# Pool mixers as products with scaled band matrices, turned tiles in two FFNs, and the last store on SyncE

## The chip, the cores and the metric

The kernel runs on one core of one Trainium2 chip. The metric is the device time of one execution in microseconds. Matrix products run on TensorE (PE in the profile), elementwise work on VectorE (DVE), ScalarE (ACT) and GpSimd (POOL); SyncE (SP) issues the loads. Each engine has its own queue of instructions, worked off in order, and they meet only at semaphores.

## The reference

One inference step of a trunk of 4 layers, for a prompt of 512 tokens and 8 sample tokens of one token each, 1024 channels, float32. Each layer is x = x + mixer(rmsnorm(x)) and x = x + swiglu(rmsnorm(x)). The mixers are pool, convolution, attention, pool. The pool mixer, which the change rewrites, is

```
u = rmsnorm(x, g)                       # rows; 15 rows of history come before a sample token
for group g, window w in (2, 4, 8, 16): # 4 groups of 256 channels
    mean = mean of the last w rows of u (of those there are)
    d[g] = mean - u
    y[g] = d[g] @ pool_w[g]             # 256 x 256
x = x + y * scale
state_p = last 15 rows of u (prompt);  state_s = history and u, last 15 rows (samples)
```

`swiglu(h)` is `(silu(h @ w_gate) * (h @ w_up)) @ w_down` with 2816 inner channels. The outputs are x at the end, for prompt and samples, the states of the pool and convolution layers, and rows of keys and values.

## The kernel before

**Layout.** x is kept with channels on partitions: 8 tiles of 128 channels by 520 tokens (512 of the prompt, then 8 samples). A float32 matrix product is made from three products of a faster type: both factors are split in a high and a low part, and low by low is left out (`half_products`, L487). A weight comes as `raw` (512 KB, loaded by SP), ScalarE makes `w_hi` (L925) and VectorE `w_lo` (L1264). A **unit** is the part of a weight that one slot holds, 48 products of 260 columns. The other factor is made likewise: after a tile of x is updated, ScalarE makes its square (L931) and the next input's `xin_hi` (L940), VectorE `xin_lo` (L1276), and POOL adds the squares up (L1738). `means` (L515) averages them over channels by products with a constant matrix, and ScalarE makes 1/rms by Ln and Exp (L945, L946), the same in all partitions, `rstd`.

**Order.** Every engine's program is written out by hand, in the same order of units and tiles; tables (`UNIT`, `TILE`, `TP`, `MIX`, `STORED`) give the counts that the waits use. `TP` numbers the **batches** of turned data: TensorE turns a tile by a product with the identity (`batch`, L534; `tails`, L566) into `bank6` or `bank7`, ScalarE copies it out (L950), and the next batch in that bank waits for that copy.

**Start.** SP loads the constants (561 KB), the samples, x in two halves of the channels, the weights of the first mixer and the history. POOL loads 15 rows of vectors (gains, biases), which are turned too, into `vec`. TensorE turns samples and 8 tiles of x, ScalarE copies and squares, VectorE adds up squares (L1700), `means(0)` and `rstd` follow, then `vec`.

**Pool mixer.** VectorE makes `hn` = x * gain * rstd, 8 tiles (L1287). The sample columns go with the turned history (L1293 to L1300). The window sums of `hn` are made by adding shifted copies, groups 0 and 1 on VectorE (L1313), 2 and 3 on POOL (`window_sums`); VectorE makes the difference to `hn` (L1321 to L1323). ScalarE rounds it to `mix_hi` (L970), VectorE makes `mix_lo` (L1329), and TensorE makes the group's 48 products, 24 for each tile of output. VectorE updates x (L1338), and the next input follows as above. TensorE also turns the last 23 columns of `hn` (L566) into `stage`, from which POOL stores the states.

**FFN.** 44 units for gate and up, two slots each step, and then 8 tiles of the down product with 3 units each. In the fourth FFN the output tile is turned by `y_tile`, tile c - 1 after tile c of four, and at the fourth tile of four both the third and the fourth:

```
                        if layer == 3:
                            if c:
                                y_tile(m0, i, c - 1)
                            if c == 3:
                                y_tile(m0, i, 3)
```

ScalarE copies it to `y_sb` (L950), and POOL stores it, 256 KB of the prompt (L1871) and 4 KB of the samples (L1874) a tile.

## Time and profile before

| | |
|---|---|
| median of 3 runs | 2254.21 us (2250.06 to 2254.46) |
| the profiled execution | 2252.45 us |
| its span | 2250.2 us |
| TensorE busy | 2102.0 us, 93% |
| VectorE, ScalarE, POOL busy | 1079.6, 952.1, 326.5 us |
| mean granted clock of TensorE | 0.975 of 2.4 GHz |
| MB, mean 90 GB/s |

Durations are read from the profiled execution; its time is 2.25 us more than its span. A row of a timeline has a start, a duration, the engine, the line of the kernel, the operation, what is written and read, and a count of instructions that follow one another; in brackets stands how long the engine was idle before, and what ended that. The records of products overlap, since they are pipelined: two that start 0.12 us apart are each 0.28 long. A float32 product that isn't split stands in the trace as two records.

### The profile page before, as it was taken

Reading aid. Unit: us, or ns where it says so; the run is one execution under the profiler, and the core shown is the slowest. Engines: PE = TensorE matmul, PEld = TensorE weight load, DVE = VectorE, ACT = ScalarE, POOL = GpSimd, SP = SyncE. Lnnn points to the kernel's source line nnn. Section 1 sums busy time; section 2 is a strip of 40 time slices with the busy share of each in tenths; the row PEclk is TensorE's granted clock in tenths of the full one; section 3 lists DMA queues with packets and bytes.
Section 4 is the critical chain, followed back from the end, with each engine's and each line's share of the span. In section 5 each row is a group of like instructions: output and inputs, shape, how many; then the busy total and the mean of one; then the engine's idle time right before and its main releaser. Section 6 shows DMA issues by size and latency. Waiting matters only on the chain. (4 is left out here: it accounts for less than half of the span.)

```text
span 2250.2 us, 41629 instructions
## 1 busy us (share of the span) xinstructions
PE 2102.0 (93%) x17072; PEld 2029.2 (90%) x17072; DVE 1079.6 (48%) x1446; ACT 952.1 (42%) x1280; POOL 326.5 (15%) x294
## 2 busy tenths in 40 slices
PE   2899999999889999999899979999999949999998
PEld 1899999999369999999899959999999939999998
DVE  5644443359955444433366655444432284444321
ACT  3543432255764434322477753443432234343221
POOL 4200000048921000000111114000000140000000
PEclk9999999999899999999999989999999969999999
DMA  4233332342003333322433252333332313333231
GB/s 135 68 92 93 93 90 86 96 103 75 29 22 89 90 93 93 91 86 77 150 113 102 69 205 76 88 93 93 90 89 87 88 30 91 87 92 93 87 106 52
DMA packets 345054, 201.53 MB, mean 90 GB/s; under 512 B 7465, under 2 KB 337481, under 8 KB 344932
## 3 DMA queue, kind: packets, MB, share of 16 engines
q1 hardware_dynamic: 341460, 193.21, 29.1%
q0 software_dynamic: 3504, 7.06, 1.1%
q8 instruction: 64, 1.05, 0.2%
q14 instruction: 26, 0.21, 0.0%
HBM read 193.51 MB, written 8.60 MB: 90 GB/s over the span
## 5 line engine op out<-in xcount | busy, mean ns | idle before, releaser
L487 PE MATMUL acc<-xin_hi,w_hi 128*128 128x260 f32 x3456 | 984.1, 285 | 11.0 <-issue 6.9
L487 PE MATMUL acc<-xin_hi,w_lo 128*128 128x260 f32 x3456 | 978.5, 283 | 0.0
L487 PE MATMUL acc<-xin_lo,w_hi 128*128 128x260 f32 x3456 | 975.5, 282 | 0.0
L925 ACT ACTIVATE w_hi<-raw 128x1024 fp32r<-128x1024 f32 (+1 forms) x332 | 344.9, 1039 | 992.1 <-PE acc L487 974.9
L487 PEld LDWEIGHTS acc<-xin_hi,w_hi 128*128 128x128 f32 x3456 | 652.4, 189 | 22.9 <-issue 17.9
L487 PEld LDWEIGHTS acc<-xin_lo,w_hi 128*128 128x128 f32 x3456 | 652.0, 189 | 0.3
L487 PEld LDWEIGHTS acc<-xin_hi,w_lo 128*128 128x128 f32 x3456 | 652.2, 189 | 0.0
L1264 DVE TENSOR_TENSOR w_lo<-raw,w_hi 128x1024 fp32r<-128x1024 f32 (+1 forms) x332 | 406.3, 1224 | 351.5 <-ACT w_hi L925 351.5
L487 PE MATMUL acc<-h_hi,w_hi 128*128 128x260 f32 x1408 | 397.9, 283 | 0.0
L487 PE MATMUL acc<-h_lo,w_hi 128*128 128x260 f32 x1408 | 397.9, 283 | 0.0
L487 PE MATMUL acc<-h_hi,w_lo 128*128 128x260 f32 x1408 | 397.5, 282 | 0.0
L487 PEld LDWEIGHTS acc<-h_hi,w_lo 128*128 128x128 f32 x1408 | 265.3, 188 | 0.0
L487 PEld LDWEIGHTS acc<-h_hi,w_hi 128*128 128x128 f32 x1408 | 264.9, 188 | 0.4 <-issue 0.3
L487 PEld LDWEIGHTS acc<-h_lo,w_hi 128*128 128x128 f32 x1408 | 264.9, 188 | 0.0
L1382 DVE TENSOR_TENSOR u_buf<-acc,rstd 128x520 f32<-128x520 f32 x88 | 61.6, 700 | 293.9 <-PE acc L487 293.9
L1379 DVE TENSOR_TENSOR g_buf<-acc,rstd 128x520 f32<-128x520 f32 x88 | 61.6, 700 | 227.9 <-PE acc L487 215.0
L487 PE MATMUL acc<-mix_hi,w_hi 128*128 128x260 f32 x320 | 98.2, 307 | 46.8 <-DVE x L1338 15.6
L1738 POOL TENSOR_TENSOR sqacc<-sqacc,sq 128x520 f32<-128x520 f32 x49 | 83.5, 1704 | 386.3 <-ACT sq L931 386.0
L1813 POOL TENSOR_TENSOR conv<-conv,prod_p 128x512 f32<-128x512 f32 x90 | 131.4, 1461 | 33.2 <-ACT prod_p L1031 21.3
L1735 POOL COPY sqacc<-sq 128x520 f32<-128x520 f32 x7 | 6.8, 966 | 870.8 <-ACT sq L931 870.8
L487 PEld LDWEIGHTS acc<-mix_hi,w_hi 128*128 128x128 f32 x320 | 66.3, 207 | 50.1 <-issue 47.2
L487 PE MATMUL acc<-mix_lo,w_hi 128*128 128x260 f32 x320 | 96.1, 300 | 0.0
(281 smaller groups left out, 1977.4 us busy)
## 6 DMA issues: line engine op xcount, KB each, us to landing
raw<-in_ffn_w_gate SPq DMA_DIRECT2D x88, 512.0 KB, 3.9
raw<-in_ffn_w_up SPq DMA_DIRECT2D x88, 512.0 KB, 3.9
raw<-in_ffn_w_down SPq DMA_DIRECT2D x64, 512.0 KB, 4.1
raw<-in_ffn_w_down SPq DMA_DIRECT2D x32, 384.0 KB, 3.5
raw<-in_attn_w_qkv SPq DMA_DIRECT2D x24, 512.0 KB, 3.9
raw<-in_conv_w_in SPq DMA_DIRECT2D x16, 512.0 KB, 4.0
raw<-in_conv_w_out SPq DMA_DIRECT2D x8, 512.0 KB, 4.1
in_mix<-in_cache_k SPq DMA_DIRECT2D x8, 512.0 KB, 5.1
```

Source lines behind the costliest of these rows:

```text
L487: last = pe.matmul(acc[:, b, 0:HALF], w[:, w_tile * P:(w_tile + 1) * P], v[:, h * HALF:(h + 1) * HALF], start=start and t == 0, stop=stop ...
L925: act.activation(w_hi[n.slot(2)][:, 0:cols], raw[:, n.slot(4), 0:cols], ACT.Copy).then_inc(split_hi, 1)
L1264: dve.tensor_tensor(w_lo[n.slot(2)][:, 0:cols], raw[:, n.slot(4), 0:cols], w_hi[n.slot(2)][:, 0:cols].bitcast(F32), ALU.subtract).then_inc ...
L1379: dve.tensor_tensor(halves(g_buf[:, c, :]), accumulator(m), halves(rstd[:]), ALU.mult).then_inc(evacuated, 1)
L1382: dve.tensor_tensor(halves(u_buf[:]), accumulator(m + 1), halves(rstd[:]), ALU.mult).then_inc(evacuated, 1)
L1735: pool_e.tensor_copy(sqacc[:], sq[:, 0, :]).then_inc(sq_added, 1)
L1738: pool_e.tensor_tensor(sqacc[:], sqacc[:], sq[:, m % 2, :], ALU.add).then_inc(sq_added, 1)
L1813: pool_e.tensor_tensor(out, out, prod_p[:, p % 3, :], ALU.add).then_inc(prod_added, 1)
```

## The change

A pool mixer no longer normalizes x in its layout by channels. It takes x with **tokens on partitions**, in 4 blocks of 128 tokens (the rows as they come from memory for the first mixer; for the second, tiles that TensorE turns in the third FFN). A window mean minus the token is a product over tokens with a **band matrix**: for a window it holds 1/w on w diagonals, less 1 on the main one, 128 rows by 128 + 16 columns, the last for what reaches into the next block. The 1/rms of a token is a factor of a row of that matrix, so the band matrices are scaled by it, four blocks by four windows. The gain of a channel is applied when the product is copied out as `mix_hi` and `mix_lo`. Edge, history and samples have small matrices of their own.

- **SP**: 64 KB of the constants first, x in four blocks of tokens, the band matrices (360 KB); the other constants last. Bands and history of the second mixer are loaded in the third FFN, ahead of that mixer's weights. SP issues the stores of the last output tile.
- **1/rms of tokens**: the first mixer squares and sums rows of x (two blocks and the samples on ScalarE, two on VectorE); in the second `token_means` makes 5 small products. Then Sqrt on ScalarE and a reciprocal on VectorE. The root of blocks 0 and 1 scales bands on ScalarE, 2 and 3 on VectorE.
- **TensorE**: `bands(m)` for a tile of 128 channels, 4 products of 128 columns and 3 of w columns, unsplit float32, into one of two banks; `samples()`, 16 products of 8 columns; the groups' products as before. The order is bands 0, 1, samples, bands 2, 3, group 0, bands 4, 5, group 1, bands 6, 7, groups 2, 3. In the first mixer the turns of the tiles 5 to 7 of x (`start_tile`) stand between.
- **VectorE**: `hn`, sample sums, window sums and differences go. It scales bands, makes `mix_lo` by tile, and two rows of state of 1024 elements, which POOL stores. POOL's window sums go, too. The first sum of squares and `means(0)` go; scalars for attention are made in the first FFN.
- **Third and fourth FFN**: tile c - 1 is turned after the first of the three units of tile c (`turn_tile`), tile 7 at the end; ScalarE copies it at the end of tile c.

The core of the diff:

```diff
+        t, p = np.arange(BAND)[None, :], np.arange(P)[:, None]
+        seen = (t >= p) & (t < p + win)
+        own = (t == p).astype(np.float32)
+        bands[:, B_MAIN + BAND * g:B_MAIN + BAND * (g + 1)] = np.where(seen, 1.0 / win, 0.0) - own
+        bands[:, B_EDGE + 16 * g:B_EDGE + 16 * g + 16] = (np.where(seen, 1.0 / np.minimum(t + 1, win), 0.0) - own)[:, 0:16]
+        for b in range(DEC):
+            bands[HIST_P * b + HIST_P - (win - 1):HIST_P * (b + 1), B_HIST + DEC * g + b] = 1.0 / win
+            bands[b, B_SMP + DEC * g + b] = 1.0 / win - 1.0
...
+            sp.dma_start(const[:, 0:P], shape_constants[:, 0:P]).then_inc(ident_in, 16)
+            sp.dma_start(xs_rows[:], x_sample[:, 0, :]).then_inc(rows_in[4], 16)
+            for b in range(4):
+                sp.dma_start(x_rows[:, b, :], x_prompt[0, b * P:(b + 1) * P, :]).then_inc(rows_in[b], 16)
+            sp.dma_start(band_c[:], shape_constants[:, N_CONST:N_CONST + N_BAND]).then_inc(bands_in, 16)
             load_pool(0)
             sp.dma_start(hist_rows[:], state_pool[0].rearrange("b j d -> (b j) d")).then_inc(hist_in, 16)
+            for rows in (slice(0, DEC), slice(96, P)):
+                sp.dma_start(gain_rows[rows, :], norm_mix[0].partition_broadcast(rows.stop - rows.start)).then_inc(gains_in[0], 16)
+            sp.dma_start(const[:, P:N_CONST], shape_constants[:, P:N_CONST]).then_inc(consts_in, 16)
...
+            sp.wait_ge(units_done, UNIT["ffn2"] + 2 * FT)
+            sp.dma_start(band_l[:], shape_constants[:, N_CONST:N_CONST + N_BAND]).then_inc(bands_in, 16)
+            sp.dma_start(hist_l[:], state_pool[1].rearrange("b j d -> (b j) d")).then_inc(hist_in, 16)
             load_pool(1)
...
             load_ffn(3)
+            tb = TP["end"] + 2 * (KT - 1)
+            sp.wait_ge(tp_taken, tb + 1)
+            sp.dma_start(y_prompt[0].rearrange("(b p) c -> p b c", p=P)[:, :, D - P:D],
+                         y_sb[:, KT - 1, 0:SEQ].rearrange("p (b c) -> p b c", b=4)).then_inc(last_stored, 16)
+            sp.wait_ge(tp_taken, tb + 2)
+            sp.dma_start(y_sample[:, 0, D - P:D], y_sb[0:DEC, KT - 1, SEQ:SEQ + P]).then_inc(last_stored, 16)
...
+            def token_means():
+
+                pe.wait_ge(sq_added, 8 * 6)
+                pe.wait_ge(rstd_ready, 6)
+                for b in range(4):
+                    pe.matmul(pair[:, 1, 2 * b:2 * b + 2], sqacc[:, b * P:(b + 1) * P], avg[:, 0:2], start=True, stop=True)
+                pe.matmul(pair[0:DEC, 1, 8:10], sqacc[:, SEQ:T], avg[:, 0:2], start=True, stop=True).then_inc(mean_ready, 1)
...
+                def bands(m):
+                    g, win = m // 2, WINDOWS[m // 2]
+                    if m < 2:
+                        pe.wait_ge(band_act, 2 * q + 2)
+                        pe.wait_ge(band_dve, 3 * q + 3)
+                    else:
+                        pe.wait_ge(mix_lo_ok, mix + m - 1 + (m > 3))
+                    cols = slice(m * P, (m + 1) * P)
+                    for b in range(4):
+                        last = pe.matmul(pair[:, m % 2, b * P:(b + 1) * P], x_tok[:, b, cols], band_s[:, b, g, 0:P],
+                                         start=True, stop=b == 0)
+                        if b:
+                            last = pe.matmul(pair[:, m % 2, b * P:b * P + win], x_tok[:, b - 1, cols], band_s[:, b - 1, g, P:P + win],
+                                             start=False, stop=True)
+                    last.then_inc(band_full, 1)
+
+                def samples():
+                    pe.wait_ge(hist_in, 16 if q == 0 else 64)
+                    pe.wait_ge(bands_in, 16 * q + 16)
+                    pe.wait_ge(tp_taken, TP["end"] if q else 3)
+                    for m in range(KT):
+                        cols, here = slice(m * P, (m + 1) * P), DEC * (m // 2)
+                        pe.matmul(bank7[:, DEC * m:DEC * (m + 1)], xs_tok[0:DEC, cols], smp_diag[:, here:here + DEC],
+                                  start=True, stop=True)
+                        last = pe.matmul(bank7[:, 64 + DEC * m:64 + DEC * (m + 1)], hist[:, cols],
+                                         band[0:DEC * HIST_P, B_HIST + here:B_HIST + here + DEC], start=True, stop=True)
+                    last.then_inc(smp_full, 1)
...
+                if q:
+                    token_means()
+                bands(0)
+                bands(1)
+                samples()
+                bands(2)
+                bands(3)
+                if q == 0:
+                    pe.wait_ge(smp_ready, 1)
+                    start_tile(7, 5, bank7, 3)
+                group(0)
+                if q == 0:
+                    start_tile(8, 6, bank6, 7)
+                bands(4)
+                bands(5)
+                group(1)
+                if q == 0:
+                    start_tile(9, 7, bank7, 8)
+                bands(6)
+                bands(7)
+                group(2)
+                group(3)
...
+                            if layer >= 2 and j == 0 and i + c:
+                                turn_tile(layer, m0, 4 * i + c - 1)
...
+                def high(m):
+                    act.wait_ge(band_full, 8 * q + m + 1)
+                    act.activation(mix_hi[:, m, 0:SEQ], pair[:, m % 2, :], ACT.Copy, scale=vec[:, gain + m:gain + m + 1])\
+                       .then_inc(mix_hi_ok, 1)
...
+                    act.activation(tok[0:DEC, ROOT + 4:ROOT + 5], pair[0:DEC, 1, 8:9], ACT.Sqrt, bias=eps[0:DEC]).then_inc(root_ready, 1)
+                act.wait_ge(rstd_ready, 6 * q + 1)
+                act.wait_ge(bands_in, 16 * q + 16)
+                main = band[:, B_MAIN:B_MAIN + 4 * BAND].rearrange("p (g t) -> p g t", g=4)
+                act.activation(band_s[:, 0, :, 16:BAND], main[:, :, 16:BAND], ACT.Copy, scale=tok[:, RSTD:RSTD + 1])
+                act.activation(band_s[:, 0, :, 0:16], band[:, B_EDGE:B_EDGE + 64].rearrange("p (g t) -> p g t", g=4), ACT.Copy,
+                               scale=tok[:, RSTD:RSTD + 1]).then_inc(band_act, 1)
+                act.activation(band_s[:, 1], main, ACT.Copy, scale=tok[:, RSTD + 1:RSTD + 2]).then_inc(band_act, 1)
...
+                def low(m):
+                    dve.wait_ge(mix_hi_ok, mix + m + 1 + (m > 1))
+                    dve.scalar_tensor_tensor(mix_lo[:, m, 0:SEQ], pair[:, m % 2, :], vec[:, gain + m:gain + m + 1],
+                                             mix_hi[:, m, 0:SEQ].bitcast(F32), ALU.mult, ALU.subtract).then_inc(mix_lo_ok, 1)
...
+                dve.wait_ge(root_ready, q + 1)
+                dve.reciprocal(tok[:, RSTD:RSTD + 4], tok[:, ROOT:ROOT + 4])
+                dve.reciprocal(tok[0:DEC, RSTD + 4:RSTD + 5], tok[0:DEC, ROOT + 4:ROOT + 5]).then_inc(rstd_ready, 1)
+                dve.wait_ge(rstd_ready, 6 * q + 1)
+                dve.wait_ge(bands_in, 16 * q + 16)
+                main = band[:, B_MAIN:B_MAIN + 4 * BAND].rearrange("p (g t) -> p g t", g=4)
...
+                for b in range(2, 4):
+                    dve.tensor_scalar(band_s[:, b], main, tok[:, RSTD + b:RSTD + b + 1], None, ALU.mult).then_inc(band_dve, 1)
+                low(0)
+                low(1)
...
+                                       vec[:, gain:gain + KT].unsqueeze(2).to_broadcast([P, KT, DEC]), ALU.mult))
+                dve.tensor_tensor(smp_diff[:], smp_own[:], bank7[:, 64:128].rearrange("p (k b) -> p k b", k=KT), ALU.add)\
...
+                                                 accum_out=lam_tmp[:, QK + j:QK + j + 1]).then_inc(lam_sums, 1)
+                        dve.wait_ge(lam_sums, j + 1)
+                dve.wait_ge(gains_in[q], 32)
+                if q == 0:
+                    dve.wait_ge(rows_in[4], 16)
+                else:
+                    dve.wait_ge(tp_taken, TP["end"])
+                x_tok, xs_tok, _, _, out = POOL_IN[q]
+                for here, rows, col in ((slice(96, P), x_tok[96:P, 3, :], 3), (slice(0, DEC), xs_tok[:], 4)):
+                    dve.scalar_tensor_tensor(out[here, :], rows, tok[here, RSTD + col:RSTD + col + 1], gain_rows[here, :],
+                                             ALU.mult, ALU.mult).then_inc(state_ready, 1)
+                update(0)
+                update(1)
+                low(4)
+                low(5)
+                low_next(0)
+                low_next(1)
+                update(2)
+                update(3)
+                low(6)
+                low(7)
+                low_next(2)
+                low_next(3)
+                for m in (4, 6):
+                    update(m)
+                    update(m + 1)
+                    low_next(m)
+                    low_next(m + 1)
...
+                pool_e.dma_start(pool_state_p[q, 0], out[P - HIST_P:P, :]).then_inc(stored, 16)
+                pool_e.dma_start(pool_state_s[q, :, HIST_P - 1, :], out[0:DEC, :]).then_inc(stored, 16)
 
```

What the order of VectorE's instructions is at the start of the second mixer, before (`hn`, then the sample columns, window sum and difference of the first group):

```order
L1284 MEMSET hn 128x8x16 [waits rstd_ready]
L1285 MEMSET wsum 128x4x16
L1287 SCALAR_TENSOR_TENSOR hn<-x,vec,rstd 128x520 x8
L1293 COPY hist_s<-hn 128x64 [waits tp_taken,hn_ready,pads_ready]
L1296 TENSOR_REDUCE last_s<-hist_s 128x16 [waits dve_seq]
L1296 TENSOR_REDUCE last_s<-hist_s 128x16 x3
L1300 SCALAR_TENSOR_TENSOR diff<-last_s,hn 128x2x8 [waits dve_seq]
L1300 SCALAR_TENSOR_TENSOR diff<-last_s,hn 128x2x8 x3
L1313 TENSOR_TENSOR wsum<-hn 128x2x512
L1321 TENSOR_TENSOR edge<-wsum,const 128x32 [waits dve_seq]
L1322 TENSOR_TENSOR diff<-edge,hn 128x2x16 [waits dve_seq]
L1323 SCALAR_TENSOR_TENSOR diff<-wsum,hn 128x2x496
```

and in the changed kernel, up to the first update of x:

```order
L1477 RECIPROCAL tok<-tok 128x4 [waits root_ready]
L1478 RECIPROCAL tok<-tok 8x1
L1482 TENSOR_SCALAR smp_diag<-band_l,tok 8x32 [waits bands_in,rstd_ready]
L1485 TENSOR_SCALAR band_s<-band_l,tok 128x576 x2
L1450 SCALAR_TENSOR_TENSOR mix_lo<-pair,vec,mix_hi 128x512 [waits mix_hi_ok] x2
L1491 TENSOR_TENSOR smp_own<-bank,vec 128x64 [waits smp_full]
L1493 TENSOR_TENSOR smp_diff<-smp_own,bank 128x64 [waits dve_seq]
L1497 TENSOR_TENSOR mix_lo<-smp_diff,mix_hi 128x8x8 [waits mix_hi_ok,smp_ready]
L1450 SCALAR_TENSOR_TENSOR mix_lo<-pair,vec,mix_hi 128x512 [waits mix_hi_ok] x2
L1516 SCALAR_TENSOR_TENSOR rows_l<-x_turned,tok,gain_rows 32x1024 [waits tp_taken,gains_in1]
L1516 SCALAR_TENSOR_TENSOR rows_l<-xs_l,tok,gain_rows 8x1024
L1461 SCALAR_TENSOR_TENSOR x<-acc,vec,x 128x520 [waits tile_done] x2
```

The work on whole tiles of x is gone, and low parts and state rows stand in its place ahead of the first update. TensorE at the same place, before (the means, turned history, the turned last columns of `hn`, the first group):

```order
L515 MATMUL pair<-sqacc,avg 128x260 [waits rstd_ready,sq_added]
L515 MATMUL pair<-sqacc,avg 128x260
L534 MATMUL bank<-const,hist_rows 128x120 [waits tp_taken,hist_in]
L534 MATMUL bank<-const,hist_rows 128x120 x3
L534 MATMUL bank<-const,hist_rows 128x120 [waits tp_taken]
L534 MATMUL bank<-const,hist_rows 128x120 x3
L566 MATMUL bank<-const,hn 23x128 [waits tp_taken,hn_ready]
```

and now (the turned last tile of x, the means per token, the first band tile):

```order
L700 MATMUL bank<-const,x 128x128 [waits tp_taken,evacuated]
L700 MATMUL bank<-const,x 128x128 x3
L703 MATMUL bank<-const,x 8x128 [waits tp_taken]
L574 MATMUL pair<-avg,sqacc 128x2 [waits rstd_ready,sq_added]
L574 MATMUL pair<-avg,sqacc 128x2 x3
L575 MATMUL pair<-avg,sqacc 8x2
L590 MATMUL pair<-band_s,x_turned 128x128 [waits band_dve,band_act]
L590 MATMUL pair<-band_s,x_turned 128x128
L593 MATMUL pair<-band_s,x_turned 128x2
L590 MATMUL pair<-band_s,x_turned 128x128
```

TensorE's wait on `hn` is gone; it waits on the scaled bands of ScalarE and VectorE. At the end of the last FFN TensorE had, before, two output tiles behind the last product:

```order
L598 MATMUL bank<-const,x_out 128x128 [waits tp_taken]
L598 MATMUL bank<-const,x_out 128x128 x3
L600 REGISTER_ALU
L601 MATMUL bank<-const,x_out 8x128 [waits tp_taken]
L594 REGISTER_ALU
L596 REGISTER_ALU [waits evacuated]
```

and now has one:

```order
L520 MATMUL acc<-h_lo,w_hi_58 128x260
L520 MATMUL acc<-h_hi,w_lo_60 128x260
L700 MATMUL bank<-const,x_out 128x128 [waits tp_taken,evacuated]
L700 MATMUL bank<-const,x_out 128x128 x3
L703 MATMUL bank<-const,x_out 8x128 [waits tp_taken]
```

The other one stands behind the first unit of the last tile.

## Rows read from the trace of the kernel before

**Rows 1.** The page, part 1: busy time of each engine, its share, its instructions.
```profile
PE 2102.0 (93%) x17072; PEld 2029.2 (90%) x17072; DVE 1079.6 (48%) x1446; ACT 952.1 (42%) x1280; POOL 326.5 (15%) x294
```
**Rows 2.** TensorE's waits, 0 to 100 us: line, what for, total, times, longest.
```profile
PE bank L566 <- DVE hn L1287: 13.5, 1, 13.5
...
PE bank L534 <- DMA x_rows<-in_x_prompt: 9.8, 1, 9.8
```
**Rows 3.** TensorE's waits, 1786 to 1900 us, with the second mixer.
```profile
PE bank L566 <- DVE hn L1287: 15.0, 1, 15.0
PE acc L487 <- issue: 10.4, 1, 10.4
```
**Rows 4.** Timeline of the second mixer: start, duration, instruction; ScalarE, POOL, VectorE.
```profile
1793.15 1.06 ACT L925 ACTIVATE w_hi<-raw 128x1024 fp32r<-128x1024 f32 x1 [3.25 <-PE acc L487]
...
1794.84 1.28 ACT L945 ACT_TABLE_LOAD   x1
...
1794.89 1.70 POOL L1738 TENSOR_TENSOR sqacc<-sqacc,sq 128x520 f32<-128x520 f32 x1 [14.07 <-ACT sq L931]
...
1801.68 13.57 DVE L1287 SCALAR_TENSOR_TENSOR hn<-x,vec,rstd 128x520 f32<-128x520 f32 x8
...
1819.63 1.21 DVE L1313 TENSOR_TENSOR wsum<-hn 128x1024 f32<-128x1024 f32 x1
...
1830.57 0.76 DVE L1338 SCALAR_TENSOR_TENSOR x<-acc,vec,x 128x520 f32<-128x520 f32 x1 [1.85 <-PE acc L487]
...
1857.01 2.46 DVE L1276 SCALAR_TENSOR_TENSOR xin_lo<-x,vec,xin_hi 128x520 fp32r<-128x520 f32 x2
```
**Rows 5.** Timeline of VectorE, first mixer: the first update of x.
```profile
60.34 0.76 DVE L1338 SCALAR_TENSOR_TENSOR x<-acc,vec,x 128x520 f32<-128x520 f32 x1 [1.98 <-PE acc L487]
```
**Rows 6.** Stretches of the second mixer: engines' busy time, granted clock, DMA share, GB/s.
```profile
core 0: us, PE busy (x) PEld busy (x) DVE busy (x) ACT busy (x) POOL busy (x), PEclk, DMA share, GB/s
...
1796.00:1827.60 31.60, 5.61 (x21) 4.00 (x21) 25.75 (x30) 6.96 (x10) 17.39 (x11) 0.50 0.30 71
1832.00:1834.00 2.00, 2.00 (x16) 2.00 (x15) 0.96 (x3) 0.83 (x3) 0.62 (x1) 0.84 0.00 0
1827.60:1857.50 29.90, 21.63 (x126) 21.05 (x126) 22.53 (x26) 14.27 (x21) 10.81 (x8) 0.74 0.06 19
```
**Rows 7.** f32 products: timeline at 1353 us; by line at 1794:1800 and 1857.5:1861 (busy us, mean ns).
```profile
1352.97 0.61 PE L842 MATMUL bank<-s_dec,select 128*128 128x1 f32 x4 [1.31 <-DVE select L1657]
1353.44 0.80 PE L846 MATMUL bank<-select,s_dec 128*128 128x128 f32 x5
...
L515 PE MATMUL pair<-sqacc,avg 128*128 128x260 f32 x4 | 2.1, 680 | 3.5 <-POOL sqacc L1738 3.5
...
L515 PE MATMUL pair<-sqacc,avg 128*128 128x260 f32 x4 | 1.1, 401 | 0.8 <-issue 0.8
```
**Rows 8.** Turned tiles by line over the span: the input's, the output's.
```profile
L534 PE MATMUL bank<-const,x_rows 128*128 128x128 f32 x32 | 8.5, 431 | 0.2
...
L598 PE MATMUL bank<-const,x_out 128*128 128x128 f32 x32 | 4.9, 276 | 1.7 <-ACT y_sb L950 1.7
```
**Rows 9.** ScalarE by line: a scaled copy of 512 elements out of PSUM.
```profile
L1131 ACT ACTIVATE mix_hi<-acc,sub_gain 128x512 fp32r<-128x512 f32 x8 | 5.2, 683 | 7.0 <-PE acc L720 7.0
```
**Rows 10.** The last vector row: POOL's issue, and the issues' KB and median us to landing.
```profile
8.90 0.48 POOL L1795 DMA_DIRECT2D vec_rows<-in_attn_subln  x1
...
vec_rows<-in_attn_subln POOLq DMA_DIRECT2D x1, 0.5 KB, 5.6
```
**Rows 11.** Timelines around turned output tiles, POOL's last issue, and landing of such stores.
```profile
2139.81 0.28 PE L487 MATMUL acc<-h_hi,w_lo 128*128 128x260 f32 x1
...
2140.59 0.28 PE L487 MATMUL acc<-h_lo,w_hi 128*128 128x260 f32 x1
...
2172.55 0.28 PE L487 MATMUL acc<-h_hi,w_lo 128*128 128x260 f32 x1
...
2174.52 0.66 PE L598 MATMUL bank<-const,x_out 128*128 128x128 f32 x4 [1.15 <-ACT y_sb L950]
...
2175.52 0.28 PE L487 MATMUL acc<-h_lo,w_hi 128*128 128x260 f32 x1
...
2243.45 0.51 POOL L1874 DMA_DIRECT2D out_y_sample<-y_sb  x1
...
out_y_sample<-y_sb POOLq DMA_DIRECT2D x8, 4.0 KB, 3.5
```

More of the change, by code:

```diff
@@ L369, in halves @@
             return t.rearrange("p (h c) -> p h c", h=2)
[L372 removed]
+        TP = {"start": 0, "conv": 10, "pool1": 16, "end": 32}
         @block.sync
@@ L1867, in _ @@
                 add_squares(6)
-            for m in range(KT):
+            for m in range(KT - 1):
                 tb = TP["end"] + 2 * m
```

442 lines of the change are left out of this document (221 added, 221 removed).

## The prediction

> **What bounds the kernel now.** I read the page first: TensorE is busy 93% of the span [rows 1]. In the FFN phases its 260-column products stand 0.12 us apart without a gap, so a change pays only where TensorE stands still, and costs where it puts work into those streams. The waits of the engine, by line, say where it stands still. In the first 100 us it waits 9.8 us for the rows of x and 13.5 for `hn` [rows 2]; in the second pool mixer 15.0 for `hn`, and 10.4 in the row called "issue", which stands ahead of the first group's products, while VectorE makes differences and low parts [rows 3]. The timeline says what fills these waits: VectorE makes `hn` for 13.57 us, then sample and window parts, and the first update of x, which needs the first group's products, starts at 1830.57 in the second mixer [rows 4] and at 60.34 in the first [rows 5]. Both mixers are a chain over VectorE.
>
> **Second mixer, to the first update.** Zero is 1793.15, where TensorE ends the third FFN and ScalarE starts its last split. In the change ScalarE does that split (1.06), a turned pair of copies and a square (0.7 each, by its 0.68 for 512 elements), and POOL its last add (1.70) [rows 4, 9]: 4.1 us. Then the means per token, 5 small f32 products. An f32 product is two records. Four records of one column take 0.61 us with the tail of the last, and five of 128 columns 0.80; the first of the five starts 0.47 after the first of the four. So records stand 0.12 us apart whatever the width, 0.235 a product [rows 7], at full clock. In the idle stretch ahead of the first group the granted clock is 0.50 [rows 6], the lower of the two levels (1.2 GHz), and the two L515 products take 2.1 us there against 1.1 later [rows 7]: twice the price. So 5 x 0.47 = 2.2, now 6.4. Two roots on ScalarE (estimate 0.2 each) and two reciprocals (about as much): 7.2. ScalarE scales two band matrices by 1/rms, 576 elements each, one in two pieces: by its 0.68 [rows 9] 1.5, now 8.7. VectorE scales the other two beside it.
>
> Now TensorE starts on the bands. A tile is 4 products of 128 columns and 3 of 2 to 16, 7 x 0.235 = 1.65 us, at the low clock 3.3. Bands 0 and 1 come after a long pause, so 6.6: 15.3. After that I take full clock, since before the change it had a mean of 0.84 between 4 and 6 us from the first group's start [rows 6]. Samples, 16 x 0.235 = 3.8: 19.1. Bands 2 and 3, 3.3: 22.4. High and low part of band 3, 0.68 on ScalarE and 0.75 on VectorE: 23.8. Group 0 needs only bands 0 and 1, and its first tile (12 products, 1.4 us) is done by then, but VectorE has two state rows of 1024 elements ahead of the first update, 1.21 each by the nearest row [rows 4]: 26.2. Before it was 37.4. **Gain 11.2.** `hn`, window sums and differences are gone from VectorE and POOL. A table load (1.28 before [rows 4]) fits under POOL's add and the means. The loads of bands and history, 840 KB, are issued in the third FFN, ahead of the mixer's weights on SP's queue, and TensorE waits for no weight in [rows 3]. POOL loads the gains for the state rows behind its last add (1.70 [rows 4]), two issues, and by the 5.6 of such loads [rows 10] they are there at about 11, needed at 23.8. POOL's two stores stand ahead of its first add and end about 1.2 after the state rows, when the first square is due.
>
> **Second mixer, from there on.** From the first update to the end of the last low part of the next input it was 1859.47 - 1830.57 = 28.9 us [rows 4]. VectorE now has 8 updates (5.6), 4 low parts (3.0), 8 low parts of the next input (9.4) and 2 splits (2.4) = 20.4, and waits, since group 3 cannot start until bands 6 and 7 went through ScalarE and VectorE. I count 7 us of waits: 27.4. **Gain 1.5.** Bounds: none, and 4.
>
> **First mixer.** It starts when `vec` is there, which high and low parts need. The last of its rows is issued by POOL at 8.90 and lands 5.6 later: 14.5 [rows 10]. The rows of x should be earlier: the constants ahead of them are now 64 KB, not 561. TensorE turns `vec` (0.7) and four tiles of x, 16 turns of 0.22 (twice the 0.11 of the output's turns, see below): 18.7. Bands 0 and 1 at low clock 6.6: 25.3. Samples 3.8, bands 2 and 3 3.3, high and low 1.4: 33.8. Then on VectorE a split with its wait 1.4, lambda sums 0.7, state rows 2.4: 38.4. Before: 60.34. **Gain 21.9**, and 1.0 behind it, as above. The sum of squares on VectorE, `means(0)` and the Ln and Exp are within this gain. The lambda scalars are now made in the first FFN, where VectorE waits for TensorE.
>
> The 32 turns of x took 431 ns each, those of the output 276 [rows 8], though TensorE was busy nearly without pause around the former; they ran at the low clock. The Trainium skill, "TensorE: Matmul & The Clock Gate", Part 4: PE-mode transpose, says that turns don't count as work for the clock; the trace agrees with it. If they did count, bands 0 and 1 of the first mixer would run at full clock and the time would be 3.3 us less, 2217.
>
> **Third FFN.** TensorE is full there, so turned tiles are added time. One pair (five turns) moves the next products by 0.54: 2140.59 less 2139.81 less two steps of 0.12 [rows 11]. Seven stand in the stream, the eighth in the gap before the mixer. **Loss 3.8.** ScalarE's 16 copies lie in its idle time. Each turn comes after a unit of 5.74 us, and its update takes 0.7, so none is late.
>
> **Fourth FFN.** At the fourth tile two tiles were turned in a row, and the second waited for ScalarE: 2175.52 less 2172.55 less two steps is 2.73, for 1.08 of work [rows 11]. The stall of 1.65 goes; at the end one tile moves from behind the last product into the stream, 0.54. **Gain 1.1.**
>
> **Tail.** POOL's last issue ends at 2243.96, behind three others of 0.8 and 0.5 in a row [rows 11]. Two issues are left at the end, by SyncE: gain 1.1 (1.3 less what the second turn hid). What follows, 6.2 us to the end of the span, holds a landing; the median of these stores is 3.5 [rows 11], and SyncE's may be as long or half of that, 0 to 1.8; I take 0.4, near none, as nothing shows a faster one. **Gain 1.5.** The Trainium skill, "DMA: Bandwidth & Descriptors", has hardware queues start sooner than POOL's; no run here shows it for a store.
>
> **Sum.** -11.2 - 1.5 - 21.9 - 1.0 + 3.8 - 1.1 - 1.5 = -34.4. The profiled run took 2252.45, so 2218.05; the median of the runs shown, 2254.21, is 1.76 more: **2220 us**. A difference of 0.2% (4.5 us) is about the least that a measurement of this kernel tells from none.
>
> **Rivals.**
> *The clock stays low through both mixers (slower).* Between bands, samples and groups TensorE waits for ScalarE and VectorE. If that holds the clock at 1.2 GHz, samples (3.8), bands 2 and 3 (3.3) and some 10 of the 18 us behind them (four bands, 96 group products) are added again on the path, 17 a mixer: the whole gain. If the first unit of the FFN runs so too, 5.7 more each: 2220 + 34 + 11 = **2265**. It decides from 17 us of added low-clock work a mixer. Against it: the clock had a mean of 0.74 from the first group on, with idle time between groups [rows 6]. Chance 0.05.
> *Low for part of them.* Samples and bands 2, 3 doubled, 7 us a mixer: **2234**. For it: that same 0.74 says that it takes long to rise, or falls between. Chance 0.13.
> *Late start.* The loads share the queues with 360 KB of bands and the pool weights, and `vec` or the last block comes at 20 to 22, not 14.5: **2226**. Chance 0.08.
> *Narrow products nearly free.* If products of 2 to 16 columns cost by their columns, 6.3 us a mixer on the path would go: **2207**. Records of one column at the same step as those of 128 speak against it [rows 7]. Chance 0.03. The Trainium skill, the same TensorE page, Back-to-back issue gap, gives such narrow products less than half the gap of 128 columns, while its LDWEIGHTS section lets the weight load set a floor; the rows side with the latter.
> *No change*, **2254**: the change moves the chain from `hn` to bands, high parts and state rows, and these give all of it back. Against it: `hn` alone is 13.57 us of the path and the whole new chain to the first update 26.2. Chance 0.03.
>
> **The numbers.** Forecast 0.68. The range takes in the bounds of the landing (1.4 below), 2.5 more behind each first update, full clock in bands 0 and 1 (-6.6) with the partly low clock above: 2212 to 2236. Faster 0.92, same 0.03, slower 0.05.
>
> **What would show it.** In the profile after: no `hn` row; first updates near 38 and 1800 (the second mixer's zero near 1774); clock low over bands 0 and 1 and full by the samples; turns in the third FFN of 276 ns with no wait; no wait at the fourth tile of the last FFN; SyncE's stores right behind the last copy. I would be wrong if the bands' records stood further apart than 0.12 at full clock, if the clock stayed at 0.50 past the samples, or if `vec` came after 16 us.

## Result: 2218.8 us, and the profile after

| | before | changed |
|---|---|---|
| median | 2252.89 us (4 runs, 2250.06 to 2254.46) | 2218.84 us (4 runs, 2215.9 to 2222.4) |
| ratio to before | | 0.9854, 95% interval 0.9841 to 0.9866 |
| profiled execution, span | 2250.2 us | 2215.9 us |

The forecast was 2220. By sections, each from one row of either trace to the next, it came out like this (ends of a section: first `u_buf` of the first FFN, `rstd` of the third, last update of x in the third, first `u_buf` of the fourth, last update of `x_out`, end of the span):

| section | before | changed | difference | forecast |
|---|---|---|---|---|
| start, first mixer | 96.59 | 74.11 | -22.5 | -22.9 |
| two FFNs, convolution, attention | 1419.57 | 1396.09 | -1.0 | 0 |
| third FFN | 1793.27 | 1773.52 | +3.7 | +3.8 |
| second mixer | 1867.38 | 1839.53 | -8.1 | -12.7 |
| fourth FFN | 2240.00 | 2210.97 | -1.2 | -1.1 |
| tail | 2250.2 | 2215.9 | -5.3 | -1.5 |

(Columns 2 and 3 are times in the trace, the difference is that of the section's length.) The total is right because errors cancelled: the second mixer gave 4.6 us less than forecast, the tail 3.8 more.

Not all of the first mixer's gain is the chain on VectorE. Before, `hn` started at 29.12:

```profile
29.12 13.57 DVE L1287 SCALAR_TENSOR_TENSOR hn<-x,vec,rstd 128x520 f32<-128x520 f32 x8
```

In the changed kernel the first product of the bands starts at 19.57, and the first update comes at 40.69 and not at 60.34. So 9.5 of these 19.6 us were won ahead of the chain, by the earlier rows of x, the sum of squares and `means(0)` that went, and the earlier `vec`; no run takes these apart. In the second mixer 1.3 us were won ahead of the chain (8.4 to 7.1 from the last update of the third FFN), and 4.4 in it (28.9 to 24.5).

The page of the changed kernel, part 1, which answers to [rows 1]:

```profile
PE 2135.3 (96%) x17370; PEld 2067.8 (93%) x17370; DVE 1029.6 (46%) x1402; ACT 949.2 (43%) x1298; POOL 290.8 (13%) x278
```

TensorE's waits in its first 100 us, which answer to [rows 2]:

```profile
PE bank L998 <- DMA vec_rows<-in_attn_subln: 5.2, 1, 5.2
PE acc L654 <- DMA x_rows<-in_x_prompt: 4.1, 4, 1.2
...
PE acc L520 <- DVE x L1461: 2.9, 1, 2.9
```

and from 1760 to 1880, which answer to [rows 3]:

```profile
PE pair L590 <- ACT band_s L1095: 2.4, 1, 2.4
PE acc L520 <- DVE x L1461: 2.1, 1, 2.1
PE acc L520 <- issue: 1.8, 1, 1.8
PE bank L700 <- ACT xs_l L1053: 1.8, 1, 1.8
```

The waits of 13 to 15 us for `hn` are gone, and no wait of these two stretches is longer than 5.2. TensorE is seldom idle in a mixer any more, and still the second one takes 66 us (1773.52 to 1839.53). The timeline of TensorE in the changed kernel's second mixer stands where [rows 4] did:

```profile
1777.08 1.05 PE L574 MATMUL pair<-avg,sqacc 128*128 128x2 f32 x8 [1.20 <-POOL sqacc L1896]
...
1780.66 1.22 PE L590 MATMUL pair<-band_s,x_turned 128*128 128x128 f32 x4 [2.39 <-ACT band_s L1095]
...
1786.72 0.59 PE L603 MATMUL bank<-smp_diag,xs_l 8*128 8x8 f32 x2
1787.24 0.60 PE L605 MATMUL bank<-band_l,hist_l 120*128 120x8 f32 x2
...
1795.02 1.20 PE L590 MATMUL pair<-band_s,x_turned 128*128 128x128 f32 x4
...
1800.99 0.57 PE L520 MATMUL acc<-mix_hi,w_hi 128*128 128x260 f32 x1
```

and that of VectorE has the first update:

```profile
1805.19 0.74 DVE L1461 SCALAR_TENSOR_TENSOR x<-acc,vec,x 128x520 f32<-128x520 f32 x1
```

The stretches of the second mixer (columns as in [rows 6]; the third number from the end is the granted clock) say where the time is:

```profile
1776.00:1778.00 2.00, 0.92 (x8) 0.92 (x8) 0.00 (x0) 1.83 (x3) 2.00 (x3) 1.00 0.47 131
1782.00:1784.00 2.00, 2.00 (x10) 2.00 (x11) 0.00 (x0) 0.16 (x1) 0.00 (x0) 0.50 0.00 0
1790.00:1792.00 2.00, 2.00 (x9) 1.90 (x9) 0.00 (x0) 0.00 (x0) 0.00 (x0) 0.50 0.00 0
1802.00:1804.00 2.00, 2.00 (x11) 2.00 (x11) 1.94 (x3) 0.00 (x0) 0.00 (x0) 0.50 0.00 0
1806.00:1808.00 2.00, 2.00 (x20) 2.00 (x19) 0.76 (x1) 2.00 (x4) 1.32 (x4) 1.00 0.30 47
```

and those of the first mixer:

```profile
24.00:26.00 2.00, 2.00 (x14) 1.87 (x14) 1.74 (x2) 1.47 (x3) 0.00 (x0) 1.00 0.57 241
...
28.00:30.00 2.00, 2.00 (x11) 1.98 (x10) 0.67 (x3) 0.63 (x2) 0.00 (x0) 0.50 0.85 221
...
38.00:40.00 2.00, 2.00 (x20) 2.00 (x19) 1.93 (x4) 0.00 (x0) 0.00 (x0) 1.00 0.50 138
```

TensorE is shown busy in all of each stretch from 1782 on, and the clock stays at 0.50 through 20 us of bands and samples. It is up by 1806, behind 260-column products that began at 1800.99. In the first mixer it was up over most of bands 0 and 1 and fell during the samples, at about 27.6. (Up to 20 us the column gives 1.00 too, but there the records stand as far apart as at the low level, 12 turned blocks in 2.56 us from 16.16 on; from 20.4 on they stand as at the full level. So for the start the spacing is the better witness.) The tail answers to [rows 11]: SyncE's two issues end at 2213.89, and 2.0 us later the span ends, where after POOL's it took 6.2. VectorE's last update:

```profile
2210.97 0.70 DVE L1579 TENSOR_TENSOR x_out<-acc,x 128x520 f32<-128x520 f32 x1 [8.73 <-PE acc L520]
```

The last issues on SyncE's queue:

```profile
2213.05 0.40 SPq L505 DMA_DIRECT2D out_y_prompt<-y_sb  x1
2213.49 0.40 SPq L508 DMA_DIRECT2D out_y_sample<-y_sb  x1
```

### The profile page after: what moved, and what is told of

It reads as the page before. It is cut to its first block, busy times and chain, and to the rows that moved or that the text cites. A ratio compares the mean times of both kernels' runs of the same rounds, so it can differ in the third digit from the quotient of the medians.

```text
span 2215.9 us, 42085 instructions
## 1 busy us (share of the span) xinstructions
PE 2135.3 (96%) x17370; PEld 2067.8 (93%) x17370; DVE 1029.6 (46%) x1402; ACT 949.2 (43%) x1298; POOL 290.8 (13%) x278
## 4 chain that ended last, share of the span: by engine, by line
PE 88%; POOL 4%; ACT 3%; DVE 3%; issue 2%; DMA 0%; POOLq 0%; ACTq 0%; DVEq 0%
PE acc L520 80%; POOL conv L1963 3%; PE pair L794 1%; PE pair L590 1%; PE bank L814 1%; PE pair L769 1%; DVE pair L1614 1%; ACT w_hi L1028 0%; PE acc L727 0%; PE pair L963 0%; PE acc L849 0%; PE bank L804 0%; ACT s_buf L1285 0%; PE acc L838 0%; PE pair L746 0%
## 5 line engine op out<-in xcount | busy, mean ns | idle before, releaser
L520 PE MATMUL acc<-mix_hi,w_lo 128*128 128x260 f32 x320 | 93.4, 292 | 0.0
```

Source lines behind the costliest of these rows:

```text
L520: last = pe.matmul(acc[:, b, 0:HALF], w[:, w_tile * P:(w_tile + 1) * P], v[:, h * HALF:(h + 1) * HALF], start=start and t == 0, stop=stop ...
```

## The experiments

Each starts from the changed kernel. Where one profile is compared, the sections matter more than the total: the middle of the program (first `g_buf` of the first FFN to the last update of x in the third), which no edit touches, was between 1699.7 and 1704.4 us long in these traces, so that totals can differ by 4.7 us for nothing that was edited. The table gives, from each trace: first update of x in the first mixer (A); first `g_buf` of the first FFN (B); last update of x in the third FFN to the first update in the second mixer (C), and to the first `g_buf` of the fourth FFN (D); last update of `x_out` to the end (E). The time is the median, with the number of runs.

| kernel | A | B | C | D | E | time |
|---|---|---|---|---|---|---|
| before | 60.3 | 91.6 | 37.3 | 69.1 | 10.2 | 2252.9 (4) |
| changed | 40.7 | 70.3 | 31.7 | 61.0 | 4.9 | 2218.8 (4) |
| e1, last store by POOL | 40.4 | 70.0 | 31.7 | 60.8 | 10.0 | 2223.1 (4) |
| e2, no narrow products | 35.6 | 65.4 | 26.6 | 55.0 | 5.0 | 2203.3 (1) |
| e3, turns ahead | 40.5 | 70.6 | 31.7 | 60.6 | 4.9 | 2217.5 (1) |
| e4, fillers in the pauses | 40.8 | 70.5 | 27.8 | 56.2 | 5.0 | 2212.1 (4) |
| e5, history apart | 38.3 | 67.9 | 28.3 | 57.1 | 5.0 | 2209.4 (1) |
| e6, state rows later | 41.0 | 72.8 | 30.5 | 61.5 | 4.9 | 2219.3 (1) |
| e7, vec by ScalarE | 37.1 | 66.8 | 31.7 | 61.0 | 4.9 | 2215.4 (1) |
| e8, e4 to e7 together | 39.5 | 70.4 | 25.1 | 54.8 | 4.9 | 2211.9 (4) |
| e9, fillers in the samples | 43.2 | 72.9 | 28.8 | 58.0 | 5.0 | 2217.6 (4) |
| e10, e9 and vec | 42.5 | 72.2 | 29.7 | 58.1 | 4.9 | 2214.6 (5) |
| e11, last store by ScalarE | 40.8 | 70.4 | 32.0 | 60.9 | 5.0 | 2217.4 (1) |
| e12, grouped | 39.4 | 69.1 | 26.2 | 54.6 | 4.9 | 2206.8 (5) |

### The tail: e1 and e11

```diff
-            for m in range(KT - 1):
+            for m in range(KT):
                 tb = TP["end"] + 2 * m
                 pool_e.wait_ge(tp_taken, tb + 1)
                 pool_e.dma_start(y_prompt[0].rearrange("(b p) c -> p b c", p=P)[:, :, m * P:(m + 1) * P],
```

(and SyncE's two stores left out.)

> The changed kernel with the stores of the last output tile issued by POOL again, all else as changed. The changed kernel ended 5.2 us after its last product started, the kernel before 10.5 us. Theory A (the end of the program waits longer for stores that POOL issued, whatever their length): the span grows by 3 to 5 us, to about 2220, with nothing moved by DMA in its last 4 us. Theory B (as predicted: only the longer issues and a slightly later landing): it grows by 0.5 to 1.5 us, to about 2217.

E is 10.0 again, all of the 5 us. That also answers what the two fewer issues were worth, since e1 has them too: 0.2 us (10.2 to 10.0), for POOL waits for ScalarE's copy anyway. POOL's issues in e1:

```profile
2211.50 0.79 POOL L2015 DMA_DIRECT2D out_y_prompt<-y_sb  x1 [9.98 <-ACT y_sb L1046]
2212.28 0.52 POOL L2018 DMA_DIRECT2D out_y_sample<-y_sb  x1
```

and how long such stores took there, from issue to landing (median us, last column):

```profile
out_y_prompt<-y_sb POOLq DMA_DIRECT2D x1, 256.0 KB, 2.7
out_y_sample<-y_sb POOLq DMA_DIRECT2D x1, 4.0 KB, 2.2
```

The second lands 2.2 us after its issue, at 2214.5, and the span ends at 2219.2: 4.7 us in which no DMA moves anything. That is what theory A had forecast. e11 has the two stores issued by ScalarE behind its last copy, and not by SyncE:

> The changed kernel with the last output tile's two stores issued by ScalarE, which makes the copy, and not by SyncE. From the last update of x_out to the end of the span it was 10.2 us in the kernel before, 10.0 in e1 (POOL), 4.9 in the changed kernel (SyncE). Theory A (late stores that POOL issued cost 5 us at the end; the other queues don't): 4.8 to 5.1. Theory B (it is SyncE's queue that is fast, for instance since SyncE itself waits for the end): 6 us or more.

5.0. So it is not SyncE that is fast; it is late stores by POOL that are followed by a long end. In the changed kernel POOL's last issue ends at 2203.3, 12.6 us before the end, and nothing of the kind follows. What the program waits for in these 4.7 us isn't shown by any row and stays open.

### The clock: e2, e3, e4

e2 leaves out the three narrow products of a band tile (`if b:` becomes `if False:`), so that its outputs lack what reaches in from the block of tokens before:

> The changed kernel without the 3 narrow products of each band tile (the first rows of a block of tokens then lack what reaches in from the block before). In the second mixer the clock stayed at 0.50 for 20 us of bands and samples. Theory N (the narrow products thin out the stream so that the clock is not raised): with 128-column products alone the granted clock rises within bands 0 and 1 or soon after them, and the first update comes some 5 us earlier than by the removed work alone. Theory S (unsplit float32 products do not raise it at all, or the samples hold it down): the clock stays at 0.50 until the first group, and only the narrow products' own time goes, 24 x 0.28 = 6.7 us over both mixers at the low clock, less at the full one: about 2212.

By A and C both mixers reach the first update 5.1 us earlier, where theory S gives 3.4. TensorE's timeline in the second mixer of e2:

```profile
1772.24 3.79 PE L590 MATMUL pair<-band_s,x_turned 128*128 128x128 f32 x16 [2.40 <-ACT band_s L1095]
1775.95 0.59 PE L603 MATMUL bank<-smp_diag,xs_l 8*128 8x8 f32 x2
...
1784.25 3.35 PE L590 MATMUL pair<-band_s,x_turned 128*128 128x128 f32 x16
1787.36 0.36 PE L520 MATMUL acc<-mix_hi,w_hi 128*128 128x260 f32 x1
```

and the stretches of the same:

```profile
1784.00:1786.00 2.00, 2.00 (x10) 2.00 (x11) 0.67 (x3) 0.26 (x1) 0.00 (x0) 0.50 0.00 0
1786.00:1788.00 2.00, 2.00 (x15) 2.00 (x15) 0.75 (x1) 1.05 (x2) 0.00 (x0) 0.74 0.00 0
1788.00:1790.00 2.00, 2.00 (x19) 2.00 (x18) 1.60 (x2) 0.33 (x1) 0.00 (x0) 1.00 0.00 0
```

It did not rise over bands 0 and 1, 3.7 us long here, nor over the samples; it rose at about 1787.0, 2.8 us into bands 2 and 3, so that group 0 starts at full clock. In the first mixer it rose within bands 2 and 3 too (at about 29.2). With nothing narrow between them, unsplit float32 products of 128 columns were followed by a rise in both mixers: theory N, but later than it said, and why bands 0 and 1 were not enough isn't shown. The gain itself doesn't decide for N. Most of it is the narrow products' own time: at the low clock a pair of tiles takes 3.7 us and not 6.06, 2.35 less, so 4.7 of the 5.1 for two pairs; theory S had them too cheap, at 3.4.

e3 sets 24 turned blocks ahead of the bands of the second mixer, where no pause interrupts them:

```diff
                     token_means()
+                    pe.wait_ge(band_act, 2 * q + 2)
+                    pe.wait_ge(band_dve, 3 * q + 3)
+                    for k in range(24):
+                        pe.transpose(pair[:, 0, (k % 4) * P:(k % 4 + 1) * P], x[:, k % 8, 0:P], ident)
```

> The changed kernel with 24 more turned blocks of 128 columns ahead of the bands of the second mixer, in one uninterrupted stream (their result is overwritten). At the low clock they take 24 x 0.21 = 5.1 us. Theory T (turned blocks count as work for the clock; in the first mixer it rose about 5 us after TensorE began on vec and x without a pause): the clock rises by the end of them, bands 0 and 1 run at 1.5 us a tile, not 3.0, and the 5.1 us are mostly given back: 2216 to 2219. Theory P (they do not count, as I wrote in the prediction): the clock stays at 0.50 until the first group and the time grows by 5.1: about 2222.

The stretches of e3's second mixer:

```profile
1782.00:1784.00 2.00, 2.00 (x11) 2.00 (x10) 0.00 (x0) 0.00 (x0) 0.00 (x0) 0.50 0.00 0
1784.00:1786.00 2.00, 2.00 (x20) 2.00 (x18) 0.00 (x0) 0.00 (x0) 0.00 (x0) 0.93 0.00 0
...
1794.00:1796.00 2.00, 2.00 (x9) 1.95 (x10) 0.45 (x2) 0.07 (x1) 0.00 (x0) 0.50 0.00 0
```

The clock rises during the turns, at about 1784.3, 2.8 us after they began, and with 4 us of added work C and the time are what they were. Theory T holds: **24 turned blocks in a row did raise the clock**, against what I wrote in the prediction and against the Trainium skill, "TensorE: Matmul & The Clock Gate", Part 4: PE-mode transpose; here the measurement decides. Then it falls again, during the samples.

e4 fills the pauses ahead of the second mixer's bands:

```diff
+            def fill(n):
+                w = w_hi[UNIT["pool1"] % 2]
+                for _ in range(n):
+                    pe.matmul(pair[:, 0, 0:HALF], w[:, 0:P], w[:, 0:HALF], start=True, stop=True)
...
+                    fill(10)
                     token_means()
+                    fill(18)
```

(and 14 ahead of the last turned tile.)

> The changed kernel with 42 products of 260 columns (fast type, result overwritten) put into the three stretches in which TensorE stands still between the end of the third FFN and the bands of the second mixer (14 ahead of the last turned tile, 10 behind it, 18 behind the means per token). Theory F (the low clock there is the price of the pause): the granted clock is 1.00 when the bands begin, bands 0 and 1 take 1.5 us a tile and samples 5, and the first update comes 5 to 9 us earlier: 2208 to 2212. Theory S (bands and samples cannot hold the clock, as in the first mixer, where it fell during the samples): bands 0 and 1 and most of the samples run at full clock, then it falls, and the gain is 4 to 6 us: 2211 to 2213. If fillers do not matter: 2217.

The stretches of e4's, over bands and in the samples:

```profile
1782.00:1784.00 2.00, 2.00 (x20) 2.00 (x19) 0.68 (x1) 0.69 (x1) 0.00 (x0) 1.00 0.03 8
1784.00:1786.00 2.00, 2.00 (x15) 1.88 (x13) 0.82 (x2) 0.69 (x1) 0.00 (x0) 0.91 0.00 0
...
1788.00:1790.00 2.00, 2.00 (x9) 1.90 (x10) 0.00 (x0) 0.00 (x0) 0.00 (x0) 0.50 0.00 0
```

C is 3.8 shorter, D 4.8, the time 2212.1 (2211.0 to 2214.7, all four below the changed kernel's fastest run of 2215.9; the intervals of the ratio touch at 0.984). So 42 products whose result nobody reads make the kernel faster, since they stand where TensorE waited anyway; of the 6.7 us between the medians, 1.9 are outside the section that was edited. The expectation for theory S is the one that came true: full clock over bands 0 and 1, then it fell, though sooner than expected, 1.6 us after the samples began.

### The samples: e5, e9

e5 takes the loop over 16 alternating products apart, 8 for the history and 8 for the tokens:

> The changed kernel with the 16 sample products split in two runs of 8: in the second mixer the history half stands behind the means per token, where TensorE waits 2.4 us for the scaled bands; in the first it stands between bands 0 and bands 1. Theory N (a long run of narrow products makes the clock fall: 3.7 us after the samples began in the first mixer, with 5 us of samples in a row): in the first mixer the clock does not fall, bands 2 and 3 take 1.5 us a tile, not 3.0, the first product of group 0 is at full clock, and the first update comes 3 to 5 us earlier. Theory S (8-column products of any grouping make it fall): no change in the first mixer. In the second mixer, where all is at the low clock anyway, 2.4 us of the waiting are used in both: together 2211 to 2213 by N, 2216 by S.

The gain is there (A 2.4, C 3.4, 2209.4), and the reason was another. The clock fell in the first mixer too, at about 25.5, and bands 2 and 3 ran at 3.0 us a tile, against what theory N had forecast. But a run of products of one kind is cheaper. TensorE's timeline in e5's first mixer has the two runs:

```profile
20.60 1.93 PE L603 MATMUL bank<-band_c,hist_rows 120*128 120x8 f32 x16
22.39 0.69 PE L590 MATMUL pair<-band_s,x_rows 128*128 128x128 f32 x4
...
24.02 2.29 PE L609 MATMUL bank<-smp_diag,xs_rows 8*128 8x8 f32 x16
```

and that of the changed kernel the alternating ones, at full clock too:

```profile
24.18 0.39 PE L605 MATMUL bank<-band_c,hist_rows 120*128 120x8 f32 x2
24.50 0.38 PE L603 MATMUL bank<-smp_diag,xs_rows 8*128 8x8 f32 x2
24.82 0.39 PE L605 MATMUL bank<-band_c,hist_rows 120*128 120x8 f32 x2
```

16 records of history take 1.79 us, 0.224 a product; alternating, a product takes 0.315. At the low clock it is 0.43 against 0.52. In the first mixer that is 1.4 us of A's 2.4 (samples and history take 4.0 and not 5.4); the rest is that the clock was up a little sooner. In the second, what stands between the bands is 3.5 us long and not 8.3, and the bands begin 1.4 later, behind the history: 3.4. Which difference between the two kinds of product makes alternating dearer (8 against 120 rows, or another) was not taken apart.

e9 is e4 with dense work among the samples (behind each pair two products of 260 columns in the second mixer, two turned blocks in the first):

> The fillers of e4 in the pauses ahead of the second mixer's bands, and now also fillers among the sample products of both mixers: behind each pair 2 products of 260 columns in the second mixer, 2 turned blocks of 128 columns in the first (8 x 0.24 and 8 x 0.22 us at full clock, 1.9 and 1.8 a mixer). Theory N (the samples' thin stream makes the clock fall; dense work among them holds it): clock at 1.00 from the first bands to group 0 in both mixers; bands 2 and 3 take 1.5 us a tile, group 0's first products stand 0.12 apart. Against e4 the second mixer's first update comes about 4 us earlier (23.5 after the end of the third FFN), the first mixer's about 4 earlier (36.5): 2204 to 2207. Theory S (samples and bands make it fall whatever stands among them): it falls within the samples, and the fillers' own time is added: 2213 to 2216.

2217.6, above both ranges. In the second mixer the clock holds longer than in e4, for 5.1 us of the samples (they begin at 1786.5 here) and not 1.6, and falls all the same before bands 2 and 3. The stretches of e9:

```profile
1788.00:1790.00 2.00, 2.00 (x17) 1.90 (x15) 0.08 (x1) 0.00 (x0) 0.00 (x0) 1.00 0.00 0
1790.00:1792.00 2.00, 2.00 (x14) 1.91 (x13) 0.00 (x0) 0.00 (x0) 0.00 (x0) 0.89 0.00 0
...
1794.00:1796.00 2.00, 2.00 (x10) 2.00 (x11) 0.65 (x3) 0.26 (x1) 0.00 (x0) 0.50 0.00 0
```

That the fillers held it is not shown. In the first mixers of the changed kernel, e1, e3, e4, e6 and e11, which have no filler and the same work up to there, the clock fell 1.3 to 4.3 us after the samples began, and in e9's, with turned blocks among them, after 3.9. What is shown is that this much did not keep it up, and cost its own time. More wasn't tried.

### The order on VectorE, and the start: e6, e7

> The changed kernel with VectorE's two state rows moved: in the first mixer behind its last low part, in the second behind the second update. In the first mixer they stand between low part and first update, which comes at 40.69 though the products are there at 38.1. Theory D (VectorE is the chain there, as I priced it): the first update comes 2.4 us earlier in the first mixer, up to 1.5 in the second, and some 3 us of it reach the end: 2215 to 2216. Theory G (bands, groups and the waits behind them set the pace, and VectorE's order does not matter): the first updates move, the first input of the FFN does not: 2218.

The end is as theory G says, 2219.3, but not since VectorE's order is of no matter. In the first mixer A did not move, because in this run the clock fell about 2.5 us earlier (25.0 for 27.6) and the last low part ahead of group 0 came at 38.07, not 35.55. That moment differs from run to run. Counted from that low part the first update did come 2.2 us sooner (2.9 for 5.1), and the first `g_buf` at the same 34.8: behind the mixer's last low part the state rows end at 70.8, and VectorE's lambda scalars and first `g_buf` come behind them. In the second mixer C is 1.2 shorter and D is not. So at these two new places the 2.4 us are paid again; whether another place would be free wasn't tried.

> The changed kernel with five of the 15 vector rows issued by ScalarE, which stands still then, and not as the last five by POOL. TensorE waits 5.2 us for the last of them, to 15.47. If the chain of the first mixer begins there, as I priced it: vec is there at about 12.5 (POOL's last issue ends at 6.9), and all that follows moves 2.5 to 3 us ahead: about 2216. If another load is late next (bands at about 11.5, the history at 17.7 for the samples, pool weights for group 0): less than 1 us, 2218.

A and B are 3.6 shorter: `vec` is turned at 11.9, not 15.5, and all follows. It is the one edit at the start that paid what it was priced at, and a little more (3.6 for 2.5 to 3).

### Putting them together: e8, e10, e12

> The three edits together, and the fillers of the second mixer (14 and 10, none behind the means per token, since the history half stands there). If the gains add up: fillers 6.5, samples in halves 4 or more, state rows 3, vector rows 2.5, less what overlaps: 2203 to 2206. Theory N says that in the second mixer the clock stays at 1.00 through bands 0 to 3 and group 0. Theory S says that it falls in the second half of the samples: 2208 to 2210.

2211.9, slower than either range, with four runs from 2207.3 to 2217.3. The second mixer is the best but one (D 54.8), though the clock fell at about 1780.4, within the first tile of bands, sooner than either theory had it. But the first lost what e5 and e7 had won: with `vec` 3.6 us earlier, the history run that e5 had put between bands 0 and bands 1 waited 2.2 us for its load, and the clock was at 0.50 from 20 on.

> e9 and the five vector rows by ScalarE of e7. If the gains add up, 3 us under e9: 2201 to 2204. If an earlier start meets a late load (the history lands at 17.7, the samples would begin at about 19.5), 1 us under e9 at most.

2214.6, 3 us under e9 as in the first clause, whose 2201 to 2204 had counted on e9's expected time; the section that changed, A, moved by 0.7 only, so the difference is not shown to be from there.

> What paid, without what did not: history products and sample products as two runs of 8 (in e5 such a run took 0.112 us a record at full clock where alternating operands of 8 and of 120 rows took 0.157), in the first mixer one behind the other after bands 1 (so that an earlier start does not wait for the history), in the second the history half behind the means; the fillers ahead of the second mixer; the five vector rows by ScalarE. State rows as in the changed kernel, no fillers among the samples. By sections: first input of the first FFN at about 65 to 67 (changed kernel 70.3), 54.8 to 56 from the end of the third FFN to the first input of the fourth (61.0), the rest as it was: 2204 to 2209, below e4's 2212. If the parts compete instead (clock falling sooner as in e8): 2210 to 2213.

e12 takes 2206.8 us (5 runs, 2205.8 to 2211.6; ratio to before 0.9804, interval 0.979 to 0.9817, apart from the changed kernel's 0.9841 to 0.9866): faster than both kernels. D is 54.6 as expected, B is 69.1 and not 65 to 67: the samples waited 0.7 us for the history, and their 16 products ran mostly at the low clock.

## Why the prediction was right, and where it was not

- **What bounds it**: right. `hn` and what followed on VectorE were the chain, and went. In the first mixer about half of the gain came ahead of that chain, which the forecast had in its sum as well.
- **Second mixer, up to the bands**: 7.2 us and not 8.7. "5 x 0.47 = 2.2" for the means failed (the product is 2.35, and the sum goes on with that): they took 1.2, since the clock was still up (1776:1778 at 1.00).
- **"After that I take full clock"**: the step that failed. Samples took 8.3, not 3.8, bands 2 and 3 6.0, not 3.3; the first update came at 31.7, not 26.2. I had read from [rows 6] that the clock rises within a few us once TensorE is busy; the rows were of 260-column products, and I took them for any work. In e2 and e3 it rose over 128-column work; in the changed kernel it did not rise in 20 us with narrow products between. My rival "low for part of them", with samples and bands 2 and 3 doubled, is what happened in this mixer. It added 7.2 us here and 4.3 in the first mixer. That the forecast of the total was met all the same is luck: the tail, the bands 0 and 1 of the first mixer, the means and what came behind the first updates were each cheaper than priced, and together gave these 11.5 us back.
- **"Records stand 0.12 us apart whatever the width"** [rows 7]: right for 128-column tiles with their narrow products (1.5 us at full clock, 3.0 at low, for my 1.65 and 3.3), wrong for the samples, 0.157 at full clock while the two kinds alternate and 0.112 when they don't (e5).
- **First mixer**: 40.7, not 38.4. `vec` was turned at 15.5 for my 14.5; bands 0 and 1 ran mostly at full clock (3.7 for 6.6); samples took 5.4, bands 2 and 3 6.0. Behind the first update, to the first `u_buf`, the first mixer was 1.8 us shorter than I had priced and the second 1.0.
- **Turned blocks and the clock**: wrong, by e3. The 32 turns of x before stood 0.27 us apart (8.75 us for all), with ScalarE's copies and squares between them, those of the changed kernel and of e3 0.21 at the low level, without a pause; I took the first for an uninterrupted stream. That this gap is why the clock stayed low before is likely, but no run varies it alone.
- **Third and fourth FFN**: right, to 0.1 us.
- **Tail**: both terms failed, 5.3 for 1.5. The two fewer issues that I priced at 1.1 gave 0.2 (e1). I took 0.4 for the queue, where e1 against the changed kernel shows 5.1: about 0.7 since SyncE starts and issues sooner, the rest behind the last issue; the bound of 1.8 came from the stores' landing, and the long end behind it was in the old trace too, 4.6 us between the landing (2243.45 + 2.2) and the span's end.
- **State rows** as the last link: on VectorE they were, but in e6 moving them only moved what they cost.

## What to carry to other kernels

In these traces a TensorE that was shown busy all the time stood at either level of the clock. So look up the granted clock over the very kind of products that an edit adds, and not over other ones. Short narrow products were cheaper in a run of one kind, and cheapest in a stretch where TensorE waited anyway (e5); such a wait was worth filling even with products that nobody reads (e4). The last store of a program is worth trying by a queue other than POOL's (e1, e11). And where one trace is compared with another, compare section by section: a total that is met can hold two errors.

## What the runs showed of the hardware that I had not expected

- Late stores issued by POOL are followed by 4.6 to 4.7 us without any DMA before the end (the kernel before, e1). With those by SyncE or ScalarE, DMA is still at work in the last 2 us (2214:2215 of spans that end at 2215.9 and 2215.6). From the last update to the end it is 10.0 to 10.2 us against 4.9 to 5.0.
- The granted clock stayed at 0.50 through 20 us in which the profile shows TensorE busy all the time (second mixer of the changed kernel, 1780.66 to 1800.99).
- Alternating 8-column products with 8 and 120 rows take 0.315 us each at full clock, in a run of one kind (120 rows) 0.224.
- 24 turned blocks in a row raised the clock from 0.50 to 1.00, 2.8 us after they began (e3).
